# Depthwise convolution in a hybrid encoder: two ScalarE products begin VectorE's chains, three products fold onto three, and each chunk's join moves behind the next gate

## What is computed

```python
def conformer_conv(h, w1, b1, w_dw, b_dw, ln_g, ln_b, w2, b2):
    u = jnp.einsum('bsd,de->bse', h, w1) + b1
    a, gate = jnp.split(u, 2, axis=-1)
    u = a * jax.nn.sigmoid(gate)
    u = lax.conv_general_dilated(            # causal, depthwise, 31 taps
        u, w_dw[:, None, :], window_strides=(1,), padding=[(30, 0)],
        dimension_numbers=('NWC', 'WIO', 'NWC'), feature_group_count=D_MODEL) + b_dw
    u = jax.nn.silu(layernorm(u, ln_g, ln_b))
    return jnp.einsum('bsd,de->bse', u, w2) + b2
```

## Time and profile before

| | us |
|---|---|
| median of 3 runs | 890.4 (889.68 to 891.13) |
| the profiled execution, its own time | 890.13 |
| its span in the profile | 888.4 |
| PE busy | 874.8 (98%) |
| DVE busy | 701.0 (79%) |
| ACT busy | 463.6 (52%) |
| POOL busy | 140.0 (16%) |

### The profile page before, as it was taken

The page is one execution under the profiler, slowest core; times in us unless marked ns, Lnnn a source line. Parts: engine busy times, 40 slices in busy tenths (PEclk is TensorE's granted clock), DMA queues, the critical chain, the costliest instruction groups (busy, mean ns, idle before and its releaser), DMA issues.

```text
span 888.4 us, 11879 instructions
## 1 busy us (share of the span) xinstructions
PE 874.8 (98%) x4384; PEld 741.6 (83%) x4384; DVE 701.0 (79%) x940; ACT 463.6 (52%) x672; POOL 140.0 (16%) x122
## 2 busy tenths in 40 slices
PE   8999998999999999999999999999999999999997
PEld 8888897889888888888888889988888888888886
DVE  5799999777886968686868888797776968676866
ACT  5798786346372634535373544637272644536243
POOL 1599871460000020000000050000000000000000
PEclk9999999999999999999999999999999999999999
DMA  9867723305313142322314122122313142331202
GB/s 292 213 162 170 181 57 119 142 1 190 127 63 142 47 151 80 146 105 84 142 48 166 55 83 101 48 83 108 142 47 142 50 169 80 126 126 64 72 1 95
DMA packets 49384, 98.14 MB, mean 110 GB/s; under 512 B 1571, under 2 KB 18979, under 8 KB 48453
## 3 DMA queue, kind: packets, MB, share of 16 engines
q1 hardware_dynamic: 48196, 90.06, 29.1%
q0 software_dynamic: 1008, 7.34, 4.0%
q10 hardware_dynamic: 144, 0.26, 0.1%
HBM read 88.22 MB, written 2.10 MB: 102 GB/s over the span
## 4 chain that ended last, share of the span: by engine, by line
PE 82%; DVE 14%; issue 1%; ACT 1%; DMA 1%; SPq 0%; DVEq 0%; ACTq 0%
PE ps L1400 16%; PE ps L1402 16%; PE ps L1401 16%; PE ps L1635 10%; PE ps L1633 10%; PE ps L1634 10%; DVE ps L956 8%; PE ps L1419 1%; DMA w_raw<-in_conv_w 1%; PE ps L1547 1%; PE ps L1552 1%; PE ps L1548 1%; DVE ps L951 1%; DVE tok L869 1%; DVE relu L956 1%
## 5 line engine op out<-in xcount | busy, mean ns | idle before, releaser
L1400 PE MATMUL ps<-act_hi,w_hi 128*128 128x512 f32 (+1 forms) x704 | 259.7, 369 | 1.5 <-DVE act_lo L875 1.5
L1401 PE MATMUL ps<-act_lo,w_hi 128*128 128x512 f32 (+1 forms) x704 | 258.8, 368 | 0.0
L1402 PE MATMUL ps<-act_hi,w_lo 128*128 128x512 f32 (+1 forms) x704 | 258.8, 368 | 0.0
L1635 PE MATMUL ps<-w_hi,u_lo 128*128 128x512 f32 x392 | 152.7, 390 | 0.0
L1633 PE MATMUL ps<-w_hi,u_hi 128*128 128x512 f32 x392 | 152.7, 389 | 0.0
L1400 PEld LDWEIGHTS ps<-act_hi,w_hi 128*128 128x128 f32 x704 | 132.7, 189 | 23.7 <-DVE act_lo L875 1.9
L1634 PE MATMUL ps<-w_lo,u_hi 128*128 128x512 f32 x392 | 152.5, 389 | 0.0
L1402 PEld LDWEIGHTS ps<-act_hi,w_lo 128*128 128x128 f32 x704 | 132.7, 189 | 22.1
L1401 PEld LDWEIGHTS ps<-act_lo,w_hi 128*128 128x128 f32 x704 | 132.8, 189 | 21.8
L666 ACT ACTIVATE relu<-ps 128x512 f32<-128x512 f32 x36 | 21.5, 597 | 243.0 <-PE ps L1402 243.0
L1137 DVE TENSOR_TENSOR w_lo<-w_raw,w_hi 128x1024 fp32r<-128x1024 f32 x70 | 85.1, 1221 | 58.0 <-ACT w_hi L687 58.0
(11 more groups left out here) (221 smaller groups left out, 1254.6 us busy)
## 6 DMA issues: line engine op xcount, KB each, us to landing
w_raw<-in_mlp_w SPq DMA_DIRECT2D x32, 1024.0 KB, 4.7
w_raw<-in_mlp_w SPq DMA_DIRECT2D x16, 2048.0 KB, 7.8
w_raw<-in_conv_w SPq DMA_DIRECT2D x16, 512.0 KB, 5.6
prod_a<-prod_a POOLq DMA_DIRECT2D x7, 1024.0 KB, 8.0
w_raw<-in_conv_w SPq DMA_DIRECT2D x2, 2048.0 KB, 9.7
h<-in_x SPq DMA_DIRECT2D x4, 512.0 KB, 6.6
out<-tok SPq DMA_DIRECT2D x7, 256.0 KB, 2.1
gain<-in_norm_mix SPq DMA_DIRECT2D x2, 512.0 KB, 6.3
```

What stands on the lines that cost most here:

```text
L1400: nc.tensor.matmul(dst, lh, rh, start=(n == 0), stop=False)
L1401: nc.tensor.matmul(dst, lh, rl, start=False, stop=False)
L1402: return nc.tensor.matmul(dst, ll, rh, start=False, stop=(n == count - 1))
L1635: last = nc.tensor.matmul(dst, ll, rh, start=False, stop=(f == 1 and (closes or i not in (0, 5))))
```

## The change

Per chunk 0 to 6, SHARE falls from 8 to 6 and WIDE from 4 to 3, so three products are folded onto three, and PE transposes three of them. Two other taps (BEGUN = 2) become ACT products that are written to PSUM, into the chunk's own two matmul banks, which are free once the gate product is done. They come ahead of all other products of the chunk. The first has the convolution's bias added. DVE's two chains begin by reading them (a multiply and add in place of the former L951 and L954), so DVE still has 17 steps. The join of chunk e moves from the end of chunk e to behind the gate product of chunk e+1. The places of the last chunk's products in `prod_a` change with the ring.

```diff
-SHARE = (8, 8, 8, 8, 8, 8, 8, 12)
-WIDE = 4
+SHARE = (6, 6, 6, 6, 6, 6, 6, 12)
+WIDE = 3
+BEGUN = 2
...
-        LAST_SLOT = (4, 5, 6, 7, 8, 9, 10, 11)
+        LAST_SLOT = (3, 4, 5, 9, 6, 7, 8, 10)
...
+        def begin(e, n):
+            return ps[:, 2 * (e % 2) + 1 - n, :]
...
+        def begun_taps(e):
+            return BEGUN if e < NC - 1 else 0
...
             def products(e):
                 act.wait_ge(glu_ok, e + 1)
+                for n in range(BEGUN):
+                    t = POOL_SHARE + SHARE[e] + n
+                    nc.scalar.activation(begin(e, n), upad[:, e % 2, t:t + S], ACT.Identity, scale=params[:, e, t:t + 1],
+                                         bias=0.0 if n else params[:, e, TAPS:TAPS + 1]).then_inc(begin_ok, 1)
                 pool_products(e, range(3))
...
+            def join(e):
+                nc.vector.tensor_tensor(relu[:, e % 2, :], relu[:, e % 2, :], ps[:, 7, :], ALU.add).then_inc(conv_ok, 1)
...
                                                upad[:, s, PAD:], ALU.add, ALU.mult).then_inc(glu_ok, 1)
+                if e:
+                    dve.wait_ge(dve_self, self_at[0])
+                    join(e - 1)
                 dve.wait_ge(glu_ok, e + 1)
                 sums = (ps[:, 6, :], ps[:, 7, :])
                 end = e == NC - 1
-                own = range((POOL_LAST if end else pooled_taps(e)) + SHARE[e], TAPS)
+                own = range((POOL_LAST if end else pooled_taps(e)) + SHARE[e] + begun_taps(e), TAPS)
                 for n, t in enumerate(own):
                     window, weight = upad[:, s, t:t + S], params[:, e, t:t + 1]
-                    if n >= 2:
+                    if n == 1 and e:
+                        dve.wait_ge(conv_ok, e)
+                    elif n in (2, 3) and not end:
+                        dve.wait_ge(begun_ok, BEGUN * e + n - 1)
+                    elif n >= 2:
                         dve.wait_ge(dve_self, self_at[0] - 1)
...
+                    if n < 2 and not end:
+                        dve.wait_ge(begin_ok, BEGUN * e + n + 1)
+                        nc.vector.scalar_tensor_tensor(into, window, weight, begin(e, n), ALU.mult,
+                                                       ALU.add).then_inc(begun_ok, 1)
+                        continue
...
-                dve.wait_ge(dve_self, self_at[0])
                 if end:
+                    dve.wait_ge(dve_self, self_at[0])
                     nc.vector.memset(stats[:, 4, 37:38], 0.0).then_inc(conv_ok, 1)
-                else:
-                    nc.vector.tensor_tensor(relu[:, s, :], relu[:, s, :], sums[1], ALU.add).then_inc(conv_ok, 1)
...
                     pe.wait_ge(glu_ok, e - 1)
+                    pe.wait_ge(begun_ok, BEGUN * (e - 1))
```

More of the change, by code:

```diff
@@ L185, in hybrid_encoder @@
         fold_one = [sem(f"fold_one{k}") for k in range(2)]
+        begin_ok, begun_ok = sem("begin_ok"), sem("begun_ok")
         conv_ok, conv_turned, ctok_ok = (sem(n) for n in ("conv_ok", "conv_turned", "ctok_ok"))
@@ L1468, in product_turn @@
                 pe.wait_ge(glu_ok, e)
+                pe.wait_ge(begun_ok, BEGUN * e)
                 for n in which:
```

## The result

| | median, us | runs | range |
|---|---|---|---|
| before | 890.46 | 6 | 889.68 to 891.71 |
| after | 894.36 | 6 | 893.98 to 894.83 |

The ratio is 1.0042 (95% interval 1.0031 to 1.0052): the change makes the kernel 3.9 us slower. I had forecast 891.7 with a range of 890.0 to 893.4, so the prediction was wrong: right in sign, far too small. The profiled execution of after has a span of 892.5 us, before's has 888.4.

A forecast was written before the change was run, and what follows sets the result against it. DVE bounds the kernel, with PE less than 0.1 us behind. PE's saving -0.03, chunks 1 to 6 +0.09, chunk 0 +0.80 and chunk 7 +0.47 make +1.3 us: forecast 891.7 us, range 890.0 to 893.4.

The forecast's parts named there:

- The saving on PE: Chunks 0 to 6: four transposes less each, 3.05 us in all beside DVE's chain, giving only -0.03 us directly.
- The join hides in the wait for ACT: DVE's chunks: moving the join saves 0.78 + 0.60 - 0.66, and the first step's wait for ACT's product gives it back.
- +0.47: Chunk 7: chunk 6's join ahead of the first step, which starts 1.26 us behind the gate product for 0.79.
- a shift of DVE's chunk 7 should reach the end one for one: Behind the convolution's chunks: the chain is DVE's, then PE's, without slack, so chunk 7's lateness arrives unchanged.
- rival 1: PE idles ahead of chunk 7 and its clock falls: 12% for 0.6 to 3 us, 3% for +9 us or more.
- the sum's own: DVE's chain from first gate product to chunk 7's first step: -0.03 + 0.09 + 0.80 + 0.47 = +1.3 us.
- hidden by 0.3 us: Chunk 7, after a clock fall: PE's last transposes end at 134.7, DVE reads them at 135.0.
- A: Theory entering the experiments: the new order costs some 1.3 us on DVE's chain, two clock falls do the rest.
- B: Rival theory of the experiments: the order does it all on DVE's timeline, 2.49 us late; clock falls are hidden.
- C: Rival theory of the experiments: ACT's late product in chunk 0 is most of the loss.
- The step from ACT's product to DVE: Each chunk's first DVE step: 0.035 us behind ACT's product, up to 0.13 possible; chunks 1 to 6 cost 0.015 each.
- +0.80: Chunk 0: DVE's first step waits for ACT's product behind the cast, so the chunk takes 13.555 us for 12.76.

The follow-up runs named there:

- e6: Kernel before with only the join of each chunk moved behind the next chunk's gate product: 890.86 us, ratio 0.9997.
- e4: Kernel after with the join put back at the end of its own chunk: 898.92 us, one execution.
- e3: Kernel after with 30 matmuls in place of 24 keeping PE busy in the LayerNorm stage: 893.04 us.
- e12: Kernel after, unchanged, run once more: 894.66 us.
- e15: e3 with POOL's last split of the LayerNorm stage's weights replaced by a one-input instruction: one execution, span 891.2 us.
- e9: Kernel after with 18 matmuls on PE ahead of chunk 7's first product and 30 for 24 in the LayerNorm stage: 891.29 us.
- e2: Kernel after with 18 matmuls on PE between chunk 5's transposes and chunk 7's first product: 892.45 us.
- e14: e9 with 18 matmuls in the LayerNorm stage in place of 30: 893.03 us.
- e1: Kernel after with ACT's two PSUM products ahead of the cast of chunk 2's weights in chunk 0: 891.92 us, ratio 1.0012.
- e5: Kernel after with ACT's two first products in SBUF in place of PSUM: 904.56 us, one execution.

## Why the prediction was wrong

**Right.** DVE was the bound and PE less than 0.1 us behind it (e6: PE done at the same 88.37 us). The saving on PE isn't on the path of the chunks 0 to 6. The join hides in the wait for ACT (e4: 0.72 more without that; forecast 0.78 + 0.60 - 0.66). Chunk 7's first step stands 1.25 behind its gate product, forecast 1.26, so +0.46 for +0.47. ACT's product into PSUM 0.786 for 0.77, within the bounds.

**The step that failed** is "a shift of DVE's chunk 7 should reach the end one for one", with rival 1's 12% beside it. The shift didn't end at its own size: 2.49 us at chunk 7 became 4.1 at the end of the span. So the step cost 1.6 us, and 1.2 are the sum's own (2.49 for 1.33, further down). Behind chunk 7 stand three things that react to a shift, and the chain of one execution shows none of them:

- the clock ahead of chunk 7. I had seen the mechanism and called a fall likely, but priced it as hidden by 0.3 us. PE's idle time was 4.80, not 3.3, mostly because DVE's gate product came 1.2 us later than I had it. The last transposes held DVE up by 0.2 to 1.3 us (after 0.18, e3 0.83, e12 0.90, e15 1.29);
- POOL's hold on DVE's small step. In e9 the shift loses 0.94 us there. The fall takes that back: ACT's copy of PE's sums waits for the slow transposes, and its casts, which stand behind that copy, and POOL's split, which reads them, come later. ACT's timeline in after, and then in e9:

```profile
130.72 0.59 ACT L584 COPY ctok<-ps 128x512 f32<-128x512 f32 x1 [1.58 <-PE ps L1488]
...
133.67 1.98 ACT L577 CAST w_hi<-w_raw 128x1024 fp32r<-128x1024 f32 x2
```

```profile
129.28 0.59 ACT L584 COPY ctok<-ps 128x512 f32<-128x512 f32 x1 [0.35 <-PE ps L1488]
...
132.22 1.98 ACT L577 CAST w_hi<-w_raw 128x1024 fp32r<-128x1024 f32 x2
```

  That is 1.45 us, of which 0.23 stands already at chunk 7's gate product, and POOL's split starts 1.45 later too (134.78 for 133.33). So the first fall costs some 0.2 to 1.3 directly and 0.97 by way of POOL (1.68 for 0.71);
- the clock in the LayerNorm stage. I hadn't looked there. It costs 1.35 us in the profile, and e12 has it in every execution, where before has it in about half.

Together: e9 takes 891.3. The first fall is worth 1.5 (e3 against e2 without a fall) or 1.6 (e12 against e14, another chip), the second 1.2 (within e2) or 1.6 (within the kernel before). That gives 894.0 to 894.5; measured 894.4 and 894.7 (e12). Of the theories, A has the falls right and the order's price wrong, B is refuted by e2, e3 and e9, and C holds for 1.66 us.

**The sum was too small as well.** From the gate product of chunk 0 to the first step of chunk 7 it is 92.98 us for 90.08, +2.90, where I had +1.33. Two terms were mis-sized. The step from ACT's product to DVE: 0.09 for 0.035, and DVE's first step 1.67 behind the gate product for 1.585. That is the upper part of my bound (up to 0.13 was "possible"), and with six chunks it makes +0.12 each for +0.015. I had read the gap from one pair at the LayerNorm where the instruction before DVE's was a cast. The other is chunk 0: +1.77 for +0.80, of which 0.77 is a wait of the cast for its weights. I took its start of 30.37 for a matter of ACT's row alone. It begins at 30.83 in after's profile, at 29.86 in e12's (without a wait; chunk 0 takes 13.82 there), at 30.60 in e9's. e6, made from the kernel before, has the same wait (0.76), and there DVE's first steps don't depend on it. The end of the stage is late by 2.49 rather than by 2.90 only because the first gate product came 0.41 earlier, which differs from one execution to another.

**So e9's 1.1 us near my 1.3 is luck.** The order costs 2.61 us on DVE, POOL's hold gives back 0.94, and an earlier first gate product, which nothing shows to be the change's doing, 0.84. It isn't a confirmation.

## What to carry to other kernels

When a change moves the time at which a tensor engine gets its work, list every stretch behind it where that engine idles for a microsecond or more, and treat each as a coin that can fall either way: its clock may be at the edge already in the kernel before, in half of its executions. Where an instruction of a few columns takes a microsecond, look for one of another engine that ends with it. And where an engine is the bound, look at what stands ahead of its releaser in the releaser's own row; here a cast there cost more than the product. A wait that costs nothing, as ACT's for the fold DMA, is worth a look too: in e6 it grew from 0.86 to 3.00 us and held DVE.

## What the runs showed of the hardware

- The granted clock fell behind 3.15 to 4.8 us of PE's idle time (e1, e3, e12, after), though not in every execution of e1; behind 1.29 us in about half the executions (e2), behind 1.69 in about half (before) or all (after), behind 2.66 in nine of ten (e14). Ahead of chunk 7 it came back with nothing but transposes on PE (0.50 in 124 to 127, 1.00 from 128).
- A small DVE `tensor_scalar` from SBUF to SBUF (0.17 us) waits out a POOL `tensor_tensor` or `tensor_scalar` that is running (up to 1.68 us here), and a DVE step with two SBUF tensors does too (4.45 us for 0.75 by line L979 of e5). DVE steps with one input in PSUM ran beside POOL's splits at their usual 0.66 apart (chunk 2 of before, 0.658).
- ACT's product into PSUM takes 0.03 us less than into SBUF (0.786 for 0.817, and 0.672 for 0.706 without the bias), the bias 0.11. DVE starts 0.09 to 0.10 us behind an ACT product that it waits for, in PSUM or in SBUF.
